# FF2's up stage: rows turned by block transposes and by way of HBM, and one pair of k-chunks by seven products

## The reference

```python
def conv_gated_ffn(h, w_up, conv_w, conv_b, w_down):
    u = h @ w_up                                   # 256 x 2048 by 2048 x 11264
    up_ = jnp.pad(u, ((0, 0), (1, 1), (0, 0)))
    u = up_[:, :-2] * conv_w[0] + up_[:, 1:-1] * conv_w[1] + up_[:, 2:] * conv_w[2] + conv_b
    gate, val = jnp.split(u, 2, axis=-1)
    return (jax.nn.silu(gate) * val) @ w_down      # 256 x 5632 by 5632 x 2048
```

## Time and profile before

| | us |
|---|---|
| median of three runs | 2124.97 |
| lowest, highest | 2122.83, 2125.59 |
| the profiled execution | 2125.52 |
| its span, first to last instruction | 2123.4 |
| PE busy | 2108.5 (99%) |
| DVE busy | 1738.8 (82%) |
| ACT busy | 1194.7 (56%) |

### The profile page before, as it was taken

The page is one execution under the profiler, slowest core; times in us unless marked ns, Lnnn a source line. Parts: engine busy times, 40 slices in busy tenths (PEclk is TensorE's granted clock), DMA queues, the critical chain, the costliest instruction groups (busy, mean ns, idle before and its releaser), DMA issues.

```text
span 2123.4 us, 28090 instructions
## 1 busy us (share of the span) xinstructions
PE 2108.5 (99%) x9682; PEld 1753.0 (83%) x9682; DVE 1738.8 (82%) x2498; ACT 1194.7 (56%) x1562; POOL 80.4 (4%) x114
## 2 busy tenths in 40 slices
PE   9999999999999999999999999999999999999999
PEld 7897888888888888888889878888888888888887
DVE  5889977888888887979766557569999999999787
ACT  6556675555555545545466446556666666665454
POOL 1000000001000100000000042000000000000000
PEclk9999999999999999999999999999999999999999
DMA  7665355677767767566556544466666666656665
GB/s 225 197 181 169 111 181 155 214 231 231 224 208 227 237 213 242 191 215 199 173 164 173 169 115 152 148 184 187 194 191 185 199 188 194 190 184 199 210 198 178
DMA packets 219710, 404.81 MB, mean 191 GB/s; under 512 B 14335, under 2 KB 58953, under 8 KB 219371
## 3 DMA queue, kind: packets, MB, share of 16 engines
q1 hardware_dynamic: 215755, 391.13, 59.5%
q0 software_dynamic: 3696, 11.54, 1.7%
q10 hardware_dynamic: 176, 1.06, 0.1%
HBM read 395.80 MB, written 7.86 MB: 190 GB/s over the span
## 4 chain that ended last, share of the span: by engine, by line
PE 82%; DVE 11%; issue 4%; ACT 2%; DMA 0%; DVEq 0%; ACTq 0%; POOL 0%; POOLq 0%
PE ps L679 20%; PE ps L681 20%; PE ps L680 20%; PE ps L985 6%; PE ps L986 6%; PE ps L987 6%; DVE w_lo L2075 3%; DVE gate_T L2128 2%; DVE val_T L2128 1%; PE ps L717 1%; ACT w_hi L1398 1%; DVE stage L2941 1%; DVE stage L2949 1%; DVE cv L2187 1%; PE ps L741 0%
## 5 line engine op out<-in xcount | busy, mean ns | idle before, releaser
L2075 DVE TENSOR_TENSOR w_lo<-raw,w_hi 128x1024 fp32r<-128x1024 f32 (+2 forms) x701 | 837.7, 1209 | 210.5 <-ACT w_hi L1398 204.0
L1398 ACT ACTIVATE w_hi<-raw 128x1024 fp32r<-128x1024 f32 (+2 forms) x701 | 724.6, 1045 | 459.2 <-PE ps L681 348.3
L679 PE MATMUL ps<-w_hi,hT_hi 128*128 128x512 f32 (+2 forms) x1792 | 699.8, 390 | 3.0 <-DVE w_lo L2075 2.3
L681 PE MATMUL ps<-w_hi,hT_lo 128*128 128x512 f32 (+2 forms) x1792 | 690.6, 385 | 0.0
L680 PE MATMUL ps<-w_lo,hT_hi 128*128 128x512 f32 (+2 forms) x1792 | 690.3, 385 | 0.0
L679 PEld LDWEIGHTS ps<-w_hi,hT_hi 128*128 128x128 f32 x1792 | 336.6, 188 | 72.7 <-DVE w_lo L2075 6.9
L681 PEld LDWEIGHTS ps<-w_hi,hT_lo 128*128 128x128 f32 x1792 | 336.4, 188 | 63.2
L680 PEld LDWEIGHTS ps<-w_lo,hT_hi 128*128 128x128 f32 x1792 | 336.8, 188 | 59.8
L679 PE MATMUL ps<-w_hi,aT_hi 128*128 128x512 f32 x480 | 187.1, 390 | 0.8 <-DVE w_lo L2075 0.8
L681 PE MATMUL ps<-w_hi,aT_lo 128*128 128x512 f32 x480 | 186.8, 389 | 0.0
L680 PE MATMUL ps<-w_lo,aT_hi 128*128 128x512 f32 x480 | 186.7, 389 | 0.0
(11 more groups left out here) (391 smaller groups left out, 2324.0 us busy)
## 6 DMA issues: line engine op xcount, KB each, us to landing
raw<-in_w_up SPq DMA_DIRECT2D x264, 512.0 KB, 4.2
raw<-in_w_down SPq DMA_DIRECT2D x176, 512.0 KB, 4.7
raw<-in_w_gate SPq DMA_DIRECT2D x88, 512.0 KB, 3.8
raw<-in_w_in SPq DMA_DIRECT2D x80, 464.0 KB, 3.7
raw<-in_w_out SPq DMA_DIRECT2D x64, 512.0 KB, 4.0
raw<-in_w_in SPq DMA_DIRECT2D x64, 256.0 KB, 3.2
raw<-in_w_in SPq DMA_DIRECT2D x24, 448.0 KB, 3.5
turn_rows<-stage POOLq DMA_DIRECT2D x11, 512.0 KB, 5.0
```

What stands on the lines that cost most here:

```text
L679: pe.matmul(o, xh, wh, start=first, stop=False)
L681: mm = pe.matmul(o, xl, wh, start=False, stop=last)
L1398: act.activation(w_hi[:, s, :kc, :width], raw[:, s, :kc, :width], ACT.Copy).then_inc(hi_ready, 1)
L2075: dve.tensor_tensor(w_lo[:, s, :kc, :width], raw[:, s, :kc, :width], w_hi[:, s, :kc, :width].bitcast(F32), ALU.subtract).then_inc(lo_ready, 1)
```

## The change

In FF2's loop, and in what follows it:
- Tiles come in a new order: gate pairs 0 to 7, then value pair 7, then value pairs 0 to 6 (`UP_ORDER`). Gate pair 7 and value pair 7, tiles 7 and 8, are a unit of seven products (`up_seven`), as in FF1: 189 matmuls in a turn instead of 192. DVE gets `up_combine`, `up_combine_rest`, `up_extra` and `up_value_add`, ACT gets `up_unit_hi` and a copy of bank 4, which stands behind `silu2`.
- Both halves are turned as in FF1: two block transposes (`up_blocks`) into `turn_out`, a save of 512 KB to HBM and four returns of 128 KB by POOL, then one ACT copy (`strips2`) that reorders the strips into `gate_T` or `val_T`. That is two round trips a turn. The strip transposes go.
- The combinations' buffers overlay `x_sb`. So POOL saves x to HBM (2 MB) before the loop and reads it back after the last value addition; DVE waits for both (`x_saved`, `x_back`).
- The first turn is written out ahead of the loop, which runs over turns 2 to 10. `gate_T`, taps and silu of turn j - 1 move to tiles 9 to 11 of turn j, the value's to tiles 12 and 13; `hidden_hi` and `hidden_lo` of the last turn move into DN2, to pair 6.

```diff
+UP_ORDER = [(0, i) for i in range(8)] + [(1, 7)] + [(1, i) for i in range(7)]
+UP_UNIT = 7
@@ sync
-                load_block(T_FF2, 16 * j, w_up2, [2] * 8, cols(j))
-                load_block(T_FF2 + 8, 16 * j, w_up2, [2] * 8, cols(j + FB))
+                for n, (half, i) in enumerate(UP_ORDER):
+                    load(T_FF2 + n, 16 * j, [w_up2, w_up2[:, :, DFF:]][half], 2 * i, cols(j))
@@ gpsimd, after x3
+                    pool.dma_start(x_rows, x_sb[:].rearrange("p t n -> p (t n)")).then_inc(x_saved, 16)
+                    with pool.Fori(1, FB + 1) as j:
+                        for half in range(2):
+                            pool.wait_ge(turned, FB + 2 * j - 1 + half)
+                            pool.sem_inc(pool_seen)
+                            pool.dma_start(turn_rows[half], turn_out).then_inc(turn_saved, 16)
+                            pool.wait_ge(turn_saved, 16 * (FB + 2 * j - 1 + half))
+                            pool.sem_inc(pool_seen)
+                            strips_back(half, stage[:, 1 + half].rearrange("p c s -> p (c s)"))
+                    pool.wait_ge(ff_value, 2 * (FB - 1))
+                    pool.dma_start(x_sb[:].rearrange("p t n -> p (t n)"), x_rows).then_inc(x_back, 16)
@@ tensor
             with pe.Fori(1, FB) as j:
                 pe.wait_ge(gemm_free[0], G_FF2 + j)
-                ff_tiles(T_FF2, 16 * j, 0, 0, 8)
-                pe.wait_ge(gemm_free[1], G_FF2 + j)
-                ff_tiles(T_FF2 + 8, 16 * j, 1, 0, 8)
+                for n in range(UP_UNIT):
+                    gemm_tile(T_FF2 + n, 16 * j, H, 2 * n, pair(0), n == 0, False)
+                up_seven(j)
+                for n in range(UP_UNIT + 2, 16):
+                    up_value_tile(n, j)
@@ scalar
+            def up_turn(j, after):
+
+                hi_tiles(T_FF2, 16 * j, 0, 4)
+                copy2(j - 1, 1, after)
+                hi_tiles(T_FF2, 16 * j, 4, 8)
+                up_unit_hi(j)
+                hi_tiles(T_FF2, 16 * j, 9, 10)
+                strips2(j - 1, 0, gate_T)
+                center2(j - 1, 0)
+                hi_tiles(T_FF2, 16 * j, 10, 12)
+                silu2(j - 1)
+                act.wait_ge(ff_used, 2 * UNITS1 + 2 * j)
+                act.activation(up_comb[:, 0, :], ps[:, 4, :], ACT.Copy).then_inc(ff_copied, 1)
+                hi_tiles(T_FF2, 16 * j, 12, 13)
+                strips2(j - 1, 1, val_T)
+                center2(j - 1, 1)
+                hi_tiles(T_FF2, 16 * j, 13, 15)
+                hidden_hi(j - 1)
+                hi_tiles(T_FF2, 16 * j, 15, 16)
+                copy2(j, 0, True)
...
+            up_turn(1, False)
+            with act.Fori(2, FB) as j:
+                up_turn(j, True)
             done[0] = T_DN2
-            hi_upto(T_DN2 + 2)
+            hi_upto(T_DN2 + 3)
+            copy2(FB - 1, 1, True)
+            hi_upto(T_DN2 + 8)
+            strips2(FB - 1, 0, gate_T)
             center2(FB - 1, 0)
...
+            hi_upto(T_DN2 + 10)
             silu2(FB - 1)
-            hi_upto(T_DN2 + 8)
+            hi_upto(T_DN2 + 11)
+            strips2(FB - 1, 1, val_end)
             center2(FB - 1, 1, val_end)
@@ vector
+            def up_turn(j, after):
+
+                lo_tiles(T_FF2, 16 * j, 0, 3)
+                if after:
+                    up_value_add(j - 1)
+                lo_tiles(T_FF2, 16 * j, 3, 5)
+                dve.wait_ge(gemm_free[1], G_FF2 + j)
+                dve.wait_ge(turn_saved, 16 * (FB + 2 * j - 1))
+                up_blocks(1)
+                lo_tiles(T_FF2, 16 * j, 5, 7)
+                up_combine(j)
                 lo_tiles(T_FF2, 16 * j, 7, 8)
-                taps2(j - 1, 1)
+                up_combine_rest(j)
+                lo_tiles(T_FF2, 16 * j, 9, 10)
+                taps2(j - 1, 0, parts=(0,))
+                lo_tiles(T_FF2, 16 * j, 10, 11)
+                taps2(j - 1, 0, parts=(1,))
+                lo_tiles(T_FF2, 16 * j, 11, 12)
+                up_extra(j, 0)
+                lo_tiles(T_FF2, 16 * j, 12, 13)
+                up_extra(j, 1)
+                taps2(j - 1, 1, parts=(0,))
+                lo_tiles(T_FF2, 16 * j, 13, 14)
+                taps2(j - 1, 1, parts=(1,))
                 product2(j - 1)
...
+                lo_tiles(T_FF2, 16 * j, 14, 15)
                 hidden_lo(j - 1)
+                lo_tiles(T_FF2, 16 * j, 15, 16)
                 dve.wait_ge(gemm_free[0], G_FF2 + 1 + j)
...
+                dve.wait_ge(turn_saved, 16 * (FB + 2 * j))
+                up_blocks(0)
...
+            lo_upto(T_DN2 + 3)
+            up_value_add(FB - 1)
+            lo_upto(T_DN2 + 4)
+            dve.wait_ge(gemm_free[1], G_FF2 + FB)
+            dve.wait_ge(turn_saved, 16 * (3 * FB - 1))
+            up_blocks(1)
+            lo_upto(T_DN2 + 9)
             taps2(FB - 1, 0)
...
+            lo_upto(T_DN2 + 11)
             taps2(FB - 1, 1, val_end)
+            lo_upto(T_DN2 + 12)
             product2(FB - 1)
```

More of the change, by code:

```diff
@@ L294, in build @@
         prod_s = stage[:, 1].rearrange("p c s -> p (c s)").rearrange("p (t n) -> p t n", t=TOK)
-        raw_s = gate_s
+        up_rows = [stage[:, 1 + i].rearrange("p c s -> p (c s)").rearrange("p (t n) -> p t n", t=TOK) for i in range(2)]
         prod_T = stage[:, 2].rearrange("p c s -> p (c s)")
@@ L298, in build @@
         turn_rows = nc.dram_tensor("turn_rows", (3, P, 4 * SEQ), F32, kind="Internal").ap()
+        x_rows = nc.dram_tensor("x_rows", (P, TOK * DM), F32, kind="Internal").ap()
         cg, cval = stage[:, 1], stage[:, 2]
@@ new lines, in up_value_tile @@
+            def up_value_tile(n, j):
+                c, i = T_FF2 + n, UP_ORDER[n][1]
+                pe.wait_ge(lo_ready, c + 1 + 16 * j)
+                for k in range(2):
+                    for t in range(TOK):
+                        x = [h[:, 2 * i + k, t * P:(t + 1) * P] for h in H]
+                        w = [v[:, c % RING, k, :] for v in (w_hi, w_lo)]
+                        mm = three(ps[:, 2 + t, :], x, w, i == 0 and t == 1 and k == 0, i == 6 and k == 1)
+                mm.then_inc(tile_used, 1)
@@ L2032, in hidden_hi, with up_unit_hi @@
                    .then_inc(aT_hi_ready, 1)
-            hi_upto(T_FF2 + 11)
+            def up_unit_hi(j):
+                c = T_FF2 + UP_UNIT + 1
+                act.wait_ge(raw_landed[c % RING], landed(c, 16 * j))
+                act.wait_ge(tile_used, c - RING + 1 + 16 * j)
+                act.activation(w_hi[:, c % RING, 1, :], raw[:, c % RING, 1, :], ACT.Copy).then_inc(hi_ready, 1)
+                for i in range(2):
+                    act.wait_ge(ff_ready, 2 * UNITS1 + 2 * j - 1 + i)
+                    act.activation(up_comb_hi[:, 2 * i:2 * i + 2, :], up_comb[:, 2 * i:2 * i + 2, :], ACT.Copy).then_inc(ff_hi, 1)
@@ L2679, in group_lo @@
                         turn_lo(FB - 1)
+                    if (q, p, b) == (2, 6, 1):
+                        hidden_lo(FB - 1)
                     if b == 1 and (q, p) in SUM_AT:
@@ new lines, in up_extra @@
+            def up_extra(j, part):
+                u1, u2, u3, u4 = (up_comb[:, i, :] for i in range(4))
+                if part == 0:
+                    dve.wait_ge(ff_copied, FB - 1 + j)
+                    dve.tensor_tensor(u2, ps[:, 5, :], u1, ALU.add).then_inc(ff_step, 1)
+                    dve.tensor_tensor(ps[:, 0, :], ps[:, 0, :], u1, ALU.add)
+                    dve.wait_ge(ff_step, 4 * (FB - 1) + 3 * j - 1)
+                    dve.tensor_tensor(u4, ps[:, 7, :], u2, ALU.add)
+                    dve.tensor_tensor(u3, ps[:, 6, :], u2, ALU.add).then_inc(ff_step, 1)
+                else:
+                    dve.wait_ge(ff_step, 4 * (FB - 1) + 3 * j)
+                    dve.tensor_tensor(u2, ps[:, 7, :], u3, ALU.add)
+                    dve.tensor_tensor(ps[:, 1, :], ps[:, 1, :], u3, ALU.add).then_inc(ff_added, 1)
```

164 lines of the change are left out of this document (106 added, 58 removed).

## The result

The changed kernel takes 2136.34 us (median of three runs, 2135.41 to 2139.70) against 2124.97 before: 11.4 us slower, ratio 1.006 with a 95% interval of 1.0037 to 1.0083. Its profiled execution took 2136.34 us with a span of 2134.6. The forecast was 2129.4, so the sign was right and the size 7 us short.

What follows compares the result with a forecast made beforehand. PE (busy 99%) and DVE, almost equally late in FF2, were taken as the bound. 2125.5 less 1.8 for the turns plus 6.2 for DN2's head gave 2129.9, median 0.55 lower: 2129.4 us; 8-in-10 range 2119.0 to 2142.0.

Steps and rivals of the forecast that it cites:

- the turns: FF2's ten loop turns: 43.64 us each, 436.4 against 438.2, so 1.8 us gained.
- head of DN2: Start of the second down projection: value's taps start at 25.0 to 27.6 us, PE stalls 4.3 to 6.9, 6.2 taken.
- (a): Rival, the forecast itself: slower by the head of DN2, 2129.4 us, up to 2136; chance 0.35.
- Matmuls removed: FF2's turns: seven products instead of eight save 3 matmuls a turn, 30 in ten turns, 6.8 us.
- DVE's work in a turn: FF2's turns: strip transposes go, 11.8 us is added; DVE has some 2.5 us less, near 39.2 of 42.84.
- The timetable: One FF2 turn: tile 14's split ends at 37.8, PE wants it at 37.4, a 0.4 us stall in every turn.
- Transfers: FF2's turns: combinations wait for tile 8's load, DMA share near 80%; stall 0.4 to 1.7 us a turn, 0.8 taken.
- The strips' way round: FF2's turns: last strip return lands some 12 us after the transposes; hidden, with 6 us of slack.
- Activation tables: FF2's loop: the 1.28 us table load before silu each turn and one at the loop's head both go.
- Return of x at nothing: DN2: x's return ends near 30 us after its start, is needed near 100, and was costed at nothing.
- (d): Rival: DMA-bound turns of 44.6 to 45.5 us, loads late at several tiles, 2139 to 2149 us; chance 0.10.
- (e): Rival: strips late because VectorE shuts out GpSimd in SBUF, 10 us in all, 2139 us; chance 0.02, counted with (d).

Runs made afterwards that it cites:

- copy_first: Changed kernel with one edit: ACT copies the first extra bank before silu instead of behind it; 2130.94 us, ratio 1.0023 to the kernel before.
- small trips: Changed kernel with the save and returns of the turned rows moving a quarter of their bytes, the rest left out; 2126.97 us, ratio 1.0008 to before.
- save_late: Changed kernel with the value's block transposes and save moved from before tile 5's split to behind tile 7's, after the combinations; 2159.05 us, ratio 1.0152 to before.
- gate_early: Changed kernel with the gate's strips and centres before tile 7's rounding, half its taps before the combinations; 2141.17 us, ratio 1.0075 to before.
- dn_head: Changed kernel with only DN2's head reordered: strips, centres, silu, taps and product two tiles earlier; 2136.86 us, ratio 1.0059 to before.
- dn_all: Changed kernel with dn_head's order, x returned in eight later pieces, and tile 3 rounded before the value banks' copy; 2136.22 us, ratio 1.0046 to before.
- eight: Changed kernel without its unit: tiles 7 and 8 by the usual eight products, no combinations, trips kept; 2127.28 us, ratio 1.001 to before.
- mended: Changed kernel with gate_early's move, the extra bank's copy before silu, and dn_all's three edits; 2138.65 us, ratio 1.0061 to before.

## Why the prediction was right or wrong

The sum missed by 6.9 us, and nearly all of it is one term: the turns, forecast as 1.8 gained, lost 4.6, so this term had the wrong sign. The head of DN2 came as forecast, 6.6 for 6.2. The sign of the whole was right by the head, not by my turns; that 2136.34 lies inside the range is owed to its width, since it stands just above the "up to 2136" of (a).

- **Matmuls removed, 6.8 us.** Right. The stalls at the first value tile are gone, none of the 17 stands there.
- **DVE's work in a turn.** The direction was right: busy 28 us less in ten turns, 2.8 a turn, where I had 2.5. It was idle time that grew.
- **The timetable.** Right in kind. PE waits at tile 14, six tiles after the unit, as forecast, and in seven turns at tile 13 too, which was not. The floor of 0.4 for silu before the copy is what copy_first gave back. With the small trips 0.6 a turn stays at tile 14, so the floor was 0.2 too low. What I had not seen is that tile 13 to 14 alone needs 1.25 us more than PE gives, so that a wait at tile 13 is followed by another. A turn took 44.3 us, between the 43.3 to 44 that I named as a sign of being right and the 44.5 for being wrong.
- **Transfers: the term that was mis-sized.** I bounded the stall by 0.4 and 1.7 us a turn and took 0.8, because FF1 moves as many bytes without a stall. The turns were 1.4 us each over a turn without a stall, near the high bound, of which the small trips leave 0.6. My reason was the wrong row: FF1's share is 0.71 and its trips one a turn, and a sum of bytes does not tell how long one load takes. The wait that I named, 1 to 3 us of the combinations for a load, came out at 2.4; I had it and did not carry it through the chain of 25.3 us to tile 14. Ten turns at 1.4 instead of 0.8 are 6 us, and 0.5 more was lost ahead of the first unit: that is the miss. I also had the reason too narrow: I named the value's save, and save_late showed the load as late without it.
- **Slips in the working.** The two trips move 2.1 MB a turn, not 4.2 (20.2 MB in the changed kernel's ten turns); the share worked out from FF1, 16%, did not use the 4.2 and came out at 15.8%. The low bound of the turns is 5.8 us gained, not 5.6.
- The Trainium skill's fit for one DMA ("DMA: Bandwidth & Descriptors", the anatomy of one SWDGE DMA) gives 3.2 us for 512 KB, and by it I would have kept the stall at 0.4. It is a fit for DMAs that GpSimd issues, and these loads are SP's. The traces have more for both: GpSimd's saves of 512 KB took 4.5 us (median), SP's loads 3.7 with small trips and 4.7 with full ones, tile 8's own about 6.
- **The strips' way round.** The 12 us and the slack of 6 were right: in the loop a trip took 11.0 to 13.3 us to its last landing and left 5.7 to 7.6 us of slack, but for one of 15.8, where GpSimd paused for 1.3 us between two issues. save_late and gate_early show what happens when this slack is used up.
- **Activation tables.** Right: none stands in the loop; one of 1.3 us is left in the turn written out ahead of it (at 1472.0).
- **Head of DN2.** The size was right (6.6 for 6.2), so were the taps' start (26.5 for 25.0 to 27.6) and the places of the waits. The reason was only part of it. I said that the late taps push work into a stretch without a gap, so starting them at 20.7 should heal it. dn_head started them at 20.9 and healed little. What counts is DVE's idle time while the last data are on their way: 9.4 us against 0.6, that is 8.8 more; less four groups of strip transposes of 1.78 us (7.1), more 1.2 for block transposes, 1.2 for value additions and 1.7 for gate taps that before were done ahead of DN2: 5.8 of the 6.6. Its parts are the copy ahead of tile 3 (DVE waits 2.35 us), tiles 7 and 8 (1.17 and 2.79, ACT waiting for a load and then busy with strips and centres), tile 10 (0.94) and the taps (2.09).
- **Return of x at nothing.** Half right: sending it later by itself shows nothing, but the loads beside it took up to 12.1 us in the changed kernel, where ACT waited 1.7 us for one, and 10.8 in dn_head, where with the new order it waited 4.8.
- **Rivals.** (a) has the larger part, 6.6 of 11.2. Of (d) the late loads came, but not as I had priced them: the combinations' longest wait was 2.9 us, and a turn took 44.3. `eight` shows that the DMA engines are no bound. (e) did not come: the four returns are issued in 2.2 us beside a dense DVE in all trips of the turns but the one named above.

What stays open: why `mended` loses some 2 us more in its turns than gate_early beside the stretch at half clock, or whether that is the one execution; which part of the traffic makes tile 8's load late; which term of the timetable makes the floor 0.2 too low; why only some of the long waits have a stretch at half clock behind them; and whether the last turn's data, turned by strip transposes while the other nine go by HBM, would free DN2's head; it wasn't tried.

## What to carry to other kernels

When a change puts traffic on the DMA engines, ask for each consumer how long after its release a load is wanted, not how full the engines are: splits in a ring of four had the time, the combinations, two splits after the release, did not. Then carry a wait of that consumer down its engine's queue to the next place without slack, and add up the work between two successive releases to PE there; moving the save, the taps or the product only moved the stall, because both ends were tight. A stall that has grown long can cost more than its length: look at the granted clock of the microseconds behind it, which the mean over a stage hides. And data on their way to HBM and back want other work for the engine meanwhile: at the end of this loop there was none.
